# Six pairs of gate tiles a layer as seven half-width block products with weight sums on VectorE

## The reference, cut to what matters

```python
proj = h @ w_in                                   # (288 x 1024) @ (1024 x N_IN)
...
gates = jax.nn.sigmoid(proj[..., OFF_GATE:].astype(jnp.float32)).reshape(b, L, 3, D_MODEL)
mixed = (gates[:, :, 0] * (y_hg @ w_out_hg)
         + gates[:, :, 1] * (y_ssm @ w_out_ssm)
         + gates[:, :, 2] * (y_att @ w_out_att))
out = mixed.astype(h.dtype) @ w_o
```

## Time and profile before

| what | value |
|---|---|
| runs | 2088.36, 2088.21, 2090.47 us (median 2088.36) |
| the profiled execution's own time | 2090.04 us |
| its span, first to last instruction | 2088.2 us |
| TensorE busy | 2056.7 us, 98% |
| VectorE, ScalarE, GpSimd busy | 789.0, 404.4, 157.7 us |
| granted TensorE clock | 1.0 throughout |
| the gate tiles 50 to 61, layer 0 | 249.37 to 316.39 us |
| the same tiles, layer 1 | 944.02 to 1011.04 us |

### The profile page before, as it was taken

The page is one execution under the profiler, slowest core; times in us unless marked ns, Lnnn a source line. Parts: engine busy times, 40 slices in busy tenths (PEclk is TensorE's granted clock), DMA queues, the critical chain, the costliest instruction groups (busy, mean ns, idle before and its releaser), DMA issues.

```text
span 2088.2 us, 45512 instructions
## 1 busy us (share of the span) xinstructions
PE 2056.7 (98%) x20125; PEld 1360.9 (65%) x20125; DVE 789.0 (38%) x1502; ACT 404.4 (19%) x770; POOL 157.7 (8%) x222
## 2 busy tenths in 40 slices
PE   7999999999999999999999999999999999999998
PEld 6977777778999998777777735343434444444535
DVE  5896333545676668744254310100101010101013
ACT  3423424311220143333342210000000000000000
POOL 3501020000000031112100010000000000000001
PEclk9999999999999999999999999999999999999999
DMA  5434535685554543453567699999999999999996
GB/s 168 142 105 146 167 121 153 192 269 163 149 161 147 158 143 122 128 162 110 157 187 223 257 399 411 409 412 408 411 408 411 408 411 408 405 405 400 417 406 250
DMA packets 287992, 548.79 MB, mean 263 GB/s; under 512 B 12883, under 2 KB 218501, under 8 KB 271348
## 3 DMA queue, kind: packets, MB, share of 16 engines
q1 hardware_dynamic: 279808, 535.85, 71.0%
q10 hardware_dynamic: 6644, 5.58, 0.9%
q0 software_dynamic: 1344, 4.45, 0.6%
HBM read 527.15 MB, written 22.50 MB: 263 GB/s over the span
## 4 chain that ended last, share of the span: by engine, by line
PE 93%; DMA 3%; DVE 2%; ACT 1%; issue 1%; ACTq 0%; SPq 0%; DVEq 0%
PE bank L1081 90%; DMA mem<-in_w_moe_up_dram 3%; PE bank L1087 3%; ACT mem L2070 1%; DVE mem L2561 0%; DVE mem L2898 0%; DVE mem L2565 0%; ACTq L2424 0%; DMA hv<-in_ssm_d_dram 0%; DVE hflat L2594 0%; DVE mem L2924 0%; ACTq L2427 0%; DVE col L2931 0%; DVE hflat L2561 0%; ACTq L2429 0%
## 5 line engine op out<-in xcount | busy, mean ns | idle before, releaser
L1081 PE MATMUL bank<-mem 128*32 128x256 f32 (+7 forms) x13168 | 1096.0, 388 | 9.8 <-DVE mem L2898 3.4
L1081 PEld LDWEIGHTS bank<-mem 128*32 128x32 f32 (+2 forms) x13168 | 707.0, 128 | 380.2 <-issue 222.0
L1081 PE MATMUL bank<-hflat,mem 128*128 128x288 f32 (+3 forms) x2688 | 572.8, 371 | 1.0 <-ACT hflat L2070 0.7
L1081 PEld LDWEIGHTS bank<-hflat,mem 128*128 128x128 f32 (+2 forms) x2688 | 443.3, 188 | 103.0 <-issue 12.3
L2070 ACT ACTIVATE mem<-bank 128x288 f32<-128x288 f32 (+10 forms) x421 | 179.4, 431 | 816.4 <-PE bank L1081 752.3
L1081 PE MATMUL bank<-mem,steps 128*32 128x384 f32 (+1 forms) x3072 | 290.0, 539 | 0.2 <-DMA mem<-in_w_moe_up_dram 0.2
L2561 DVE TENSOR_TENSOR mem<-mem 128x512 f32<-128x512 f32 (+10 forms) x336 | 234.6, 725 | 28.5 <-PE bank L1081 18.5
L1081 PEld LDWEIGHTS bank<-mem,steps 128*32 128x32 f32 x3072 | 100.5, 110 | 186.4 <-issue 183.5
L2565 DVE SCALAR_TENSOR_TENSOR hflat<-hflat,bank 128x512 f32<-128x512 f32 x24 | 15.1, 683 | 406.6 <-ACT hflat L2070 406.6
L2070 ACT ACTIVATE hflat<-bank 128x512 f32<-128x512 f32 (+1 forms) x40 | 19.6, 554 | 569.4 <-PE bank L1081 546.9
L2070 ACT ACTIVATE mem<-mem 128x1152 f32<-128x1152 f32 (+9 forms) x125 | 92.1, 739 | 100.3 <-DVE mem L2653 63.8
(11 more groups left out here) (249 smaller groups left out, 742.2 us busy)
## 6 DMA issues: line engine op xcount, KB each, us to landing
mem<-in_w_moe_up_dram SPq DMA_DIRECT2D x64, 2048.0 KB, 22.8
mem<-in_w_moe_down_dram SPq DMA_DIRECT2D x56, 2048.0 KB, 23.4
mem<-in_w_moe_up_dram SPq DMA_DIRECT2D x32, 2304.0 KB, 25.4
mem<-in_w_in_dram SPq DMA_DIRECT2D x70, 1024.0 KB, 5.2
mem<-in_w_moe_up_dram SPq DMA_DIRECT2D x16, 1536.0 KB
mem<-in_w_ffn_up_dram SPq DMA_DIRECT2D x44, 512.0 KB, 5.2
mem<-in_cache_kv_w_dram SPq DMA_DIRECT2D x26, 512.0 KB, 4.8
mem<-in_cache_kv_w_dram SPq DMA_DIRECT2D x74, 128.0 KB, 4.5
```

Of the source, the lines that this page charges most:

```text
L1081: return mm(out, lhsT, rhs, start=start, stop=stop, skip_group_check=True)
```

## The change

For pairs 25 to 30 (tiles 50 to 61) of both layers the two plain tiles are replaced by seven products of half width in two bank halves a and b. Two banks a pair are used in the place of one a tile. The new routines, by engine:

```diff
+GATED = (25, 26, 27, 28, 29, 30)
@@ TensorE @@
+            def gate_pair(L, t):
...
+                if t % 2 == 0:
+                    open_bank(("gate", L, p, 0))
+                    product(a[:, 0:TH], a11, hT[:, 0:h, 0:TH], True).then_inc(part_summed, 1)
+                    open_bank(("gate", L, p, 1))
+                    pe.wait_ge(*mixer_sums(L, p, 1))
+                    product(b[:, TH:T], s1, t1, True).then_inc(part_summed, 1)
+                    pe.wait_ge(*mixer_sums(L, p, 2))
+                    pe.wait_ge(*gate_kept(L, p, 1))
+                    product(a[:, 0:TH], s2, t2, False).then_inc(part_summed, 1)
+                    pe.wait_ge(*gate_kept(L, p, 2))
+                    product(b[:, 0:TH], a12, hT[:, h:KT, 0:TH], False)
+                    return
+                pe.wait_ge(*mixer_sums(L, p, 3))
+                pe.wait_ge(*gate_kept(L, p, 3))
+                product(a[:, 0:TH], a21, t3, False).then_inc(part_summed, 1)
+                pe.wait_ge(*mixer_sums(L, p, 4))
+                close_bank(product(b[:, TH:T], gsum4, hT[:, h:KT, TH:T], False), ("gate", L, p, 1))
+                pe.wait_ge(*gate_kept(L, p, 4))
+                close_bank(product(a[:, 0:TH], a22, t4, False), ("gate", L, p, 0))
+                n_slab[0] += 1
@@ ScalarE @@
+            def keep_gate(L, p, k):
+                a, b = (psum(("gate", L, p, i)) for i in range(2))
+                m = 2 * p - GATE0
+                src, to = ((a[:, 0:TH], gates[:, m, 0:TH]), (b[:, TH:T], gpart[GATED.index(p) % 2]),
+                           (a[:, 0:TH], gates[:, m, TH:T]), (a[:, 0:TH], gates[:, m + 1, TH:T]))[k - 1]
+                act.wait_ge(*gate_summed(L, p, k))
+                fn(to, src, ACT.Copy).then_inc(part_kept, 1)
+            def last_gate(L, p):
+                act.wait_ge(*filled(key))
+                empty(fn(gates[:, 2 * p - GATE0 + 1, 0:TH], psum(key)[:, 0:TH], ACT.Tanh, scale=0.5), key)
+            def summed_gates(L, p):
+                act.wait_ge(*drained(("gate", L, p, 1)))
+                fn(gates[:, m, :], gates[:, m, :], ACT.Tanh, scale=0.5)
+                fn(gates[:, m + 1, TH:T], gates[:, m + 1, TH:T], ACT.Tanh, scale=0.5)
@@ def mixer(L): @@
                     if 0 < t - AT_EVENT <= SH and (t - AT_EVENT) % 2:
                         for e in range(2):
                             ssd_decays(L, t - AT_EVENT - 1 + e)
+                    if t % 2 and p in GATED:
+                        keep_gate(L, p, 4)
...
+                    elif p in GATED and t % 2 == 0:
+                        for k in (1, 2, 3):
+                            keep_gate(L, p, k)
+                        if p - 1 in GATED:
+                            summed_gates(L, p - 1)
+                    elif p in GATED:
+                        last_gate(L, p)
@@ VectorE @@
+            def gate_weight_sums(L, p):
+                dve.wait_ge(slab_in[n % RING], 16 * slab_dmas[n])
+                if i >= 2:
+                    dve.wait_ge(*filled(("gate", L, p - 2, 0)))
...
+                tt(s1, a21, a22, ALU.add).then_inc(sums_done, 1)
+                dve.wait_ge(*mixer_sums(L, p, 1))
+                tt(s2, s1, a11, ALU.subtract).then_inc(sums_done, 1)
+                tt(a21, a11, a21, ALU.subtract).then_inc(sums_done, 1)
+            def gate_fourth_sum(L, p):
+                if i >= 1:
+                    dve.wait_ge(*filled(("gate", L, p - 1, 1)))
+                tt(gsum4, a12, gsum[i % 2][1], ALU.subtract).then_inc(sums_done, 1)
+            def join_gates(L, p):
+                dve.wait_ge(*filled(key))
+                dve.wait_ge(*gate_kept(L, p, 4))
+                v = gates[:, m + 1, TH:T]
+                step(tt(v, v, gpart[GATED.index(p) % 2], ALU.add))
+                empty(tt(gates[:, m, :], gates[:, m, :], psum(key)[:, 0:T], ALU.add), key)
+            def gate_sums_beside(L, p):
+                if p - 1 in GATED:
+                    join_gates(L, p - 1)
+                if p in GATED:
+                    gate_fourth_sum(L, p)
+                if p + 1 in GATED:
+                    gate_weight_sums(L, p + 1)
@@ def mixer(L): @@
                 hgrn_norm_out(L)
+                dve.wait_ge(stored, 16 * conv_out[L])
+                gate_weight_sums(L, GATED[0])
+                gate_sums_beside(L, GATED[0])
                 ssd_rows(L)
                 for h in range(SH + 1):
+                    if h % 2 == 0:
+                        gate_sums_beside(L, (AT_EVENT + h) // 2)
                     if h > 0 and h % 2 == 0:
                         ssd_y(L, h // 2 - 1)
                     if h < SH and h % 2 == 0:
                         ssd_head(L, h)
                         ssd_head(L, h + 1)
...
+                join_gates(L, GATED[-1])
```

More of the change, by code:

```diff
@@ L143, in hybrid_decoder @@
         gate_temp = view(arena, 14720, 4, T)
+        gsum = [[view(arena, 9496, KT // 2, P), view(arena, 10008, KT // 2, P)],
+                [view(arena, 18048, KT // 2, P), view(over, 52 * T + 256, KT // 2, P)]]
+        gsum4 = view(arena, 14136, KT // 2, P)
+        gpart = [view(arena, 10520 + TH * i, TH) for i in range(2)]
         yall = view(over, 42 * T, 10, T)
@@ L372, in plan_mixer @@
             for t in range(N_PROJ):
-                if t // 2 not in SEVEN:
+                if t // 2 not in SEVEN + GATED:
                     acc_job(("proj", L, t))
+                elif t // 2 in GATED and t % 2 == 0:
+                    for i in range(2):
+                        acc_job(("gate", L, t // 2, i))
                 elif t % 2 == 0:
@@ L608, in plan_slabs @@
             for s in range(NS_AG):
-                add_slab(("proj", L, 29 + 2 * s), (0, rows_of(w_in[L], 0, KT, OFF_ATT + 256 * s, 256)))
+                add_slab(("gate", L, 14 + s, 0) if 14 + s in GATED else ("proj", L, 29 + 2 * s), (0, rows_of(w_in[L], 0, KT, OFF_ATT + 256 * s, 256)))
             for br, w in enumerate((w_out_hgrn, w_out_ssm)):
@@ L1156, in proj_pair @@
                 n_slab[0] += 1
+            def gate_pair(L, t):
+                p, h = t // 2, KT // 2
+                if t % 2 == 0:
+                    take_slab(KT, 2 * P)
+                (a11, a12), (a21, a22) = quarters(slab(n_slab[0], KT, 2 * P))
+                t1, t2, t3, t4 = (tok_m[:, j] for j in range(4))
+                s1, s2 = gsum[GATED.index(p) % 2]
+                a, b = (psum(("gate", L, p, i)) for i in range(2))
+                if t % 2 == 0:
+                    open_bank(("gate", L, p, 0))
[17 more added lines that the diff above has]
+                n_slab[0] += 1
             def proj_slab(L, keys, nk, src):
@@ L2279, in keep_pieces @@
                         psum(key)[:, 0:n * TH])
+            def keep_gate(L, p, k):
+                a, b = (psum(("gate", L, p, i)) for i in range(2))
+                m = 2 * p - GATE0
[4 more added lines that the diff above has]
+            def last_gate(L, p):
+                key = ("gate", L, p, 0)
+                act.wait_ge(*filled(key))
+                empty(fn(gates[:, 2 * p - GATE0 + 1, 0:TH], psum(key)[:, 0:TH], ACT.Tanh, scale=0.5), key)
+            def summed_gates(L, p):
+                m = 2 * p - GATE0
+                act.wait_ge(*drained(("gate", L, p, 1)))
+                fn(gates[:, m, :], gates[:, m, :], ACT.Tanh, scale=0.5)
+                fn(gates[:, m + 1, TH:T], gates[:, m + 1, TH:T], ACT.Tanh, scale=0.5)
             def mixer(L):
```

43 lines of the change are left out of this document (34 added, 9 removed).

## The result

The changed kernel took **2103.16 us** (median of 6 runs, 2102.53 to 2104.51), the kernel before 2090.04 on the same chip (6 runs, 2088.21 to 2090.58): ratio 1.0067, 95% interval 1.0057 to 1.0077, **13.1 us slower**. The forecast was slower by 6.0, and the result lies above its range. The profiled execution has a span of 2100.5 us, 12.3 above that of before.

The account below looks back on a forecast made before the run. TensorE, busy 98% of the span, was taken as the bound. Per layer, gain -6.60 and waits 3.08 + 3.4 + 3.1 gave +3.0, both layers +6.0: median 2094.4 us, range 2090.3 to 2099.5.

Parts of the forecast that it names:

- The gain: Six pairs of gate tiles a layer: seven half-width products save 1.10 us a pair, 6.60 a layer, 13.2 in all.
- Pair 25: Gate stretch, each layer: the third product waits for the first copy, behind ScalarE's Exp of the norm, 3.08 us.
- Pair 26: Gate stretch, each layer: the seventh product waits 3.4 us for the fourth copy, behind exponentials, with VectorE 1.75 us late.
- Pairs 27 to 29: Gate stretch, each layer: seventh products wait for the fourth copy behind exponentials, 0.90, 0.98 and 1.2 us, together 3.1.
- The first part: Both gate stretches: TensorE is busy throughout, so each new wait is paid in full and each saving gained in full.
- Weight loads: Gate products: loads cost nothing, read from the dense layer's trace, against a skill rule adding some 31 us.
- the rival of paid loads: Gate products: 288 more weight loads paid at 190 ns each, +54.7 us, giving 2149 us; chance 2%.
- The shift reaches the end: After each gate stretch: its shift passes whole to the kernel's end, since later work starts on this chain's events.
- theory B: TensorE's clock, posed after the result: it falls for reasons of its own, whatever the waits; no chance given.

Follow-up runs that it names:

- the last experiment: Changed kernel with fourth copy ahead of the exponentials, norm chain taken apart, and VectorE's weight sums behind the heads for pair 27 alone: 2082.11 us, ratio 0.9969.
- The experiment that let VectorE be on time: Changed kernel with VectorE's weight sums for the next pair moved behind the two heads, in every pair: 2100.23 us, ratio 1.0056.
- the fourth copy first: Changed kernel with ScalarE's fourth copy of a pair ahead of the decay exponentials: 2092.52 us, ratio 1.0014.
- the wait ahead of the fourth product: Kernel before with an added TensorE wait for the second head's exponentials ahead of the fourth of tile 53's eight products: 2093.11 us, ratio 1.0017.
- the wait alone: Kernel before with an added TensorE wait ahead of tile 53 for the exponentials of heads 0 and 1: 2101.54 us, ratio 1.0059.

## Why the prediction was wrong, by its own steps

The direction, the places and the sizes of the waits were right; the sum was 6.0 and came out at 13.1. A layer's stretch was forecast 3.0 us longer and is 5.97 and 5.40. Two steps failed: the gain of a pair, taken too high, and the price of a wait, which had no term for the clock.

- **The gain: mis-sized, 1.2 us a layer.** The step "a pair gains 1.10 us" set two plain tiles at 3.98 us against seven products at 6.86. The 3.98 holds 0.1 us for the change to work that the row marks otherwise than 128*128. Two plain tiles back to back, with work marked 128*128 on both sides, take 7.76 in the same profile (239.67 to 247.43), 3.88 each:

```profile
239.67 7.92 PE L1081 MATMUL bank<-hflat,mem 128*128 128x288 f32 x32
247.43 2.10 PE L1081 MATMUL bank<-mem,pairs 128*128 128x288 f32 x8
```

All twelve tiles of the stretch follow this. Next to 128*128 work, transposes too, nothing is added: tile 50 takes 3.88, with transposes behind it. A neighbour with another mark (8*128, 8*64, 128*64, 128*32, 32*128) adds 0.1 on its side: tile 52, with `wdecay` behind it, takes 3.98, and a tile between two such neighbours 4.08 (305.04 to 309.12). The 6.86 stood between products of its own kind and holds none of it. In the changed kernel a product beside such work takes 1.07 or 1.08 in the place of 0.98:

```profile
266.08 1.14 PE L1103 MATMUL bank<-hflat,mem 128*128 128x144 f32 x8
267.15 0.75 PE L1103 MATMUL bank<-steps,ident 8*128 8x288 f32 x4
```

With 0.1 on each side of the small work the seven take 7.06, and the gain is 0.90, 5.4 a layer; the last experiment measured 0.85 with the short pauses left in it, so 10.2 us in both layers, not 13.2.
- **Pair 25: right.** 3.08 forecast, 3.16 measured, at P3, behind the Exp. Taking the chain apart removed it.
- **Pair 26: right.** 3.4 forecast; 3.29 in layer 0, 2.72 in layer 1, where the lost clock of the first wait had moved TensorE's part. The experiment that let VectorE be on time took off 1.6 of the 1.75 us that the step gave it.
- **Pairs 27 to 29: right,** 0.90, 0.98 and 1.2 forecast, 0.84, 0.88 and 1.03 measured. Pair 29 is not late by VectorE: its wait is 0.87 with the sums in front of the heads or behind.
- **The clock: missing from the sum, 1.7 us a layer.** The first part said that "every wait that the change brings in is paid in full". It is paid with more than that: with the longer product behind each wait, 0.5 a layer, and above all with the clock. Two waits of about 3 us stand in each layer (3.00 and 3.13, 3.00 and 2.56); behind one of them the clock fell, 1.7 us each. The waits had been worked out at 3.08 and 3.4 us and nothing was asked about what follows them. The Trainium skill, "TensorE: Matmul & The Clock Gate", section "Part 1: The HAM clock gate", says that TensorE's clock is gated by its recent activity and falls back to half rate when it idles; the trace agrees (0.57 behind the wait), and by that page there should have been a term here.
- **Weight loads: the trace's reading holds.** TensorE's products stay at 0.98 us with 57.7 us of loads beside 64.6 of products, so the rival of paid loads is out. The rule on loads that the prediction took from the Trainium skill, "TensorE: Matmul & The Clock Gate", section "Part 3: Packing small matmuls — row/col tiling", does not hold for this kernel.
- **The shift reaches the end: right,** to within the 1 us by which the part behind the experts' start differs.

The sum again, with measured terms (gain, waits, clock, longer products behind the waits): in layer 0 -5.4 + 9.2 + 1.7 + 0.5 = +6.0, for +5.97; in layer 1 -5.4 + 8.6 + 1.7 + 0.5 = +5.4, for +5.40. With the 0.9 outside of the stretches this is the 12.3 of the profile; the 13.1 of the medians differs from it by less than the runs of one kernel do. How much of that 0.9 belongs to the change is not shown. The mean clock of a run does not settle it: of the 57 runs of the kernel before, beside the experiments, ten at 1.000 took 2087.9 us on average and fourteen at 0.996 or 0.997 took 2090.1, about 2 us more, where a lower clock paid in full would be over 6.

The change could have been a gain. Its own part is worth 10 us, both layers together; the place of the fourth copy and the chain in front of the first turned it into a loss of 13, and with two orders on ScalarE mended the same products make the kernel 6.2 us faster than before.

## What to carry to other kernels

Where TensorE is busy without a break, an idle piece of some microseconds costs more than its length: look at the granted clock and at the length of a known product right behind it, and price a new wait of 2 us or more with 1.7 us on top until a trace shows otherwise. When a product is split so that another engine must answer in the middle, walk through that engine's queue for what stands in front of each answer; the step that frees the bank comes next. Take the time of an operation before and after from places with the same neighbours, since the change to work of another shape is in one row and not in the other.

## What the runs showed that was not expected

- Length alone does not decide whether the clock falls. In the profiled executions it did not fall behind any idle piece between products in the stretches of 1.69 us or less. Of fourteen from 2.18 to 3.44 us ten lost it: 2.18 (both layers), 3.13, 3.44 (both) and five of the six of 3.00 or 3.01; three of 2.48 to 2.56 and one of 3.00 did not. What else decides is open; it wasn't tried.
- Another place says the same. Near the end every profile but that of the kernel before has TensorE wait 2.00 to 3.04 us for the last weights of the experts. In nine of these eleven the clock fell behind it, also at 2.00, and the last 192 records took 12.0 to 12.3 us, as in the row of 2079.16 above. It did not fall at 2.12 (the fourth copy first) nor at 3.04 (the wait ahead of the fourth product), the row below. The kernels with only a wait added have this wait for weights too, so the seven products are not its cause; why the profile before has only 0.77 and 0.34 us there is not known.

```profile
2070.23 10.57 PE L1081 MATMUL bank<-mem 128*32 128x256 f32 x192 [3.04 <-DMA mem<-in_w_moe_down_dram]
```

- The lower clock lasted 3.41 us, or 6.83, and cost 1.7 us or, where rows can be set against it (the wait alone, and the fourth copy first, both in layer 0), 3.0.
- It also came with no idle piece of that length in front. At the start of the experts it fell in the kernel after and in the one with the norm chain taken apart; in the former TensorE is busy without a pause from 1150 us on, from 1201.85 to 1205.10 with small transposes and products of 8 columns or 1, and the clock falls right behind. At 448 us it fell in the kernel with the fourth copy first, 1.9 us behind an idle piece of 1.03. Some 14 us into the kernel it fell in five profiled executions, where TensorE is idle for a quarter of the time anyway. So theory B is out for the two stretches, where every fall came with an idle piece of 2.18 us or more, but not for the whole kernel. It varies from run to run; the 57 runs of the kernel before have mean clocks from 0.996 to 1.000 and times from 2087.1 to 2093.1 us. Why it falls at the experts in some kernels only stays open.
